# GpSimd makes the low part of more norm pieces, in a two-block float32 model on one core

## What is computed

```python
# first block
h = rmsnorm(x, norm_mix_g);  z = h @ w_in            # MIX
x = x + mixer(z) @ w_out
h = rmsnorm(x, norm_ffn_g)                           # FFN
x = x + (silu(dwconv(h @ w_gate)) * (h @ w_up)) @ w_down
x = rmsnorm(x, norm_final_g)                         # FIN1
# second block: modulate(h, shift, scale) = h * (1 + scale) + shift
h = modulate(rmsnorm(x, g0), shift0, scale0)         # POOL
x = x + gate0 * pool_mixer(h)
hk = modulate(rmsnorm(x, kv_g), shiftkv, scalekv)    # KV
k, v = hk @ w_kv
h = modulate(rmsnorm(x, g1), shift1, scale1)         # ATT, the same x
x = x + gate1 * attention(h @ b_w_in, k, v)
out = rmsnorm(x, final_g)                            # FIN2
```

## Time and profile before

| what | value |
|---|---|
| median of 3 runs | 2089.77 us (2089.43 to 2089.9) |
| the profiled execution's own time | 2088.51 us |
| its span, first to last instruction | 2086.8 us |
| TensorE busy | 2064.3 us |
| VectorE busy | 1231.7 us |
| GpSimd busy | 748.9 us |
| ScalarE busy | 650.7 us |
| mean granted TensorE clock | 0.996 |

### The profile page before, as it was taken

The page is one execution under the profiler, slowest core; times in us unless marked ns, Lnnn a source line. Parts: engine busy times, 40 slices in busy tenths (PEclk is TensorE's granted clock), DMA queues, the critical chain, the costliest instruction groups (busy, mean ns, idle before and its releaser), DMA issues.

```text
span 2086.8 us, 24768 instructions
## 1 busy us (share of the span) xinstructions
PE 2064.3 (99%) x9344; PEld 1694.1 (81%) x9344; DVE 1231.7 (59%) x1698; ACT 650.7 (31%) x1089; POOL 748.9 (36%) x441
## 2 busy tenths in 40 slices
PE   8999999999999999999999999999999999999998
PEld 7888888888888888888878888888888878777886
DVE  7999776555644456445676453453463570697565
ACT  7323345221122211222254122122121261676112
POOL 4555626222221222212276122122131462565623
PEclk9999999999999999999999999999999999999999
DMA  4231112322133222332112121121121120010202
GB/s 154 72 111 41 41 51 91 121 101 97 63 111 111 101 85 76 109 112 101 41 41 61 38 64 41 41 60 40 40 61 41 41 71 31 21 42 21 71 11 81
DMA packets 44749, 141.26 MB, mean 68 GB/s; under 512 B 5616, under 2 KB 9856, under 8 KB 44672
## 3 DMA queue, kind: packets, MB, share of 16 engines
q1 hardware_dynamic: 31632, 100.68, 15.1%
q10 hardware_dynamic: 13040, 39.54, 5.2%
HBM read 135.98 MB, written 7.36 MB: 69 GB/s over the span
## 4 chain that ended last, share of the span: by engine, by line
PE 80%; DVE 12%; POOL 4%; ACT 2%; issue 1%; DMA 0%; POOLq 0%; SPq 0%; ACTq 0%; DVEq 0%
PE psum L594 24%; PE psum L596 24%; PE psum L595 24%; DVE psum L1651 7%; POOL temp L444 2%; PE psum L932 1%; PE psum L943 1%; DVE psum L1504 1%; DVE norm_lo L1517 1%; POOL w_lo L409 1%; PE psum L911 1%; PE psum L661 1%; POOL ada_raw L444 0%; PE psum L663 0%; PE psum L662 0%
## 5 line engine op out<-in xcount | busy, mean ns | idle before, releaser
L409 POOL TENSOR_TENSOR w_lo<-w_raw,w_hi 128x1024 fp32r<-128x1024 f32 x174 | 441.6, 2554 | 972.5 <-ACT w_hi L1036 967.0
L594 PE MATMUL psum<-norm_hi,w_hi 128*128 128x512 f32 x1632 | 636.3, 390 | 0.3 <-ACT temp L1104 0.3
L596 PE MATMUL psum<-norm_hi,w_lo 128*128 128x512 f32 x1632 | 635.0, 389 | 0.0
L595 PE MATMUL psum<-norm_lo,w_hi 128*128 128x512 f32 x1632 | 634.9, 389 | 0.0
L594 PEld LDWEIGHTS psum<-norm_hi,w_hi 128*128 128x128 f32 x1632 | 306.4, 188 | 64.7 <-issue 0.9
L596 PEld LDWEIGHTS psum<-norm_hi,w_lo 128*128 128x128 f32 x1632 | 306.4, 188 | 63.8
L595 PEld LDWEIGHTS psum<-norm_lo,w_hi 128*128 128x128 f32 x1632 | 306.4, 188 | 63.3 <-issue 0.2
L1104 ACT ACTIVATE temp<-psum 128x512 f32<-128x512 f32 x160 | 93.9, 598 | 420.6 <-PE psum L596 393.7
L1567 DVE SCALAR_TENSOR_TENSOR stream<-psum,mods,stream 128x512 f32<-128x512 f32 x160 | 119.7, 750 | 172.5 <-PE psum L596 172.5
L1036 ACT CAST w_hi<-w_raw 128x1024 fp32r<-128x1024 f32 x158 | 159.2, 1047 | 138.8 <-PE psum L596 79.6
L1565 DVE TENSOR_TENSOR stream<-psum,stream 128x512 f32<-128x512 f32 x176 | 118.7, 689 | 83.8 <-PE psum L596 83.6
(11 more groups left out here) (214 smaller groups left out, 2974.7 us busy)
## 6 DMA issues: line engine op xcount, KB each, us to landing
w_raw<-in_slabs SPq DMA_DIRECT2D x175, 512.0 KB, 3.5
ada_raw<-in_ada ACTq DMA_DIRECT2D x10, 3072.0 KB, 12.6
stream<-in_x SPq DMA_DIRECT2D x8, 512.0 KB, 9.3
out<-stream SPq DMA_DIRECT2D x8, 512.0 KB, 2.8
skew_scratch<-row_scratch ACTq DMA_DIRECT2D x1, 3072.0 KB, 17.6
ada_raw<-in_ada ACTq DMA_DIRECT2D x1, 2048.0 KB, 7.9
bias<-skew_scratch ACTq DMA_DIRECT2D x4, 512.0 KB, 4.2
c_act<-in_c ACTq DMA_DIRECT2D x1, 512.0 KB, 9.7
```

The costliest lines, as they stand in the source:

```text
L409: nc.gpsimd.tensor_tensor(WL[place][:, :], RAW[at % 2][:, :], WH[place][:, :].bitcast(f32), ALU.subtract).then_inc(slab_ready, 1)
L594: nc.tensor.matmul(dst, wh, xh, start=n == 0, stop=False)
L595: nc.tensor.matmul(dst, wh, xl, start=False, stop=False)
L596: last = nc.tensor.matmul(dst, wl, xh, start=False, stop=n == len(terms) - 1)
```

## The change

GpSimd takes more pieces: FFN 7, 9, 11, 13, 15 in place of 9, 11, 13; POOL and KV 7, 9, 11, 13, 15 in place of 9, 12, 15; ATT 1, 3, 5, 7, 9, 11, 13 in place of 1, 4, 10, 13. VectorE loses as many `low` instructions. GpSimd's list is reordered to fit: piece 7 stands ahead of the first slab low part that used to come before any piece.

```diff
-        POOL_LOWS = [(MIX, m) for m in (2, 4, 6, 9, 11, 13)] + [(FFN, m) for m in (9, 11, 13)] + [(POOL, m) for m in (9, 12, 15)]
-        POOL_LOWS += [(KV, m) for m in (9, 12, 15)] + [(ATT, m) for m in (1, 4, 10, 13)]
+        POOL_LOWS = [(MIX, m) for m in (2, 4, 6, 9, 11, 13)] + [(FFN, m) for m in (7, 9, 11, 13, 15)]
+        POOL_LOWS += [(POOL, m) for m in (7, 9, 11, 13, 15)] + [(KV, m) for m in (7, 9, 11, 13, 15)]
+        POOL_LOWS += [(ATT, m) for m in (1, 3, 5, 7, 9, 11, 13)]
@@
             sums(FFN)
-            lows(FFN_SLAB + 2, FFN_SLAB + 4)
-            piece_low(FFN, 9)
-            piece_low(FFN, 11)
-            piece_low(FFN, 13)
+            lows(FFN_SLAB + 2, FFN_SLAB + 3)
+            piece_low(FFN, 7)
+            lows(FFN_SLAB + 3, FFN_SLAB + 4)
+            for m in (9, 11, 13, 15):
+                piece_low(FFN, m)
             lows(FFN_SLAB + 4, FFN_SLAB + 6)
@@
             sums(POOL, (f_lo, FT + 1))
+            piece_low(POOL, 7)
             lows(POOL_SLAB + 2, POOL_SLAB + 3)
             piece_low(POOL, 9)
+            piece_low(POOL, 11)
             lows(POOL_SLAB + 3, POOL_SLAB + 4)
-            piece_low(POOL, 12)
+            piece_low(POOL, 13)
             piece_low(POOL, 15)
@@
             sums(KV)
+            piece_low(KV, 7)
             lows(ATT_SLAB + 2, ATT_SLAB + 3)
             piece_low(KV, 9)
+            piece_low(KV, 11)
             lows(ATT_SLAB + 3, ATT_SLAB + 4)
-            piece_low(KV, 12)
-            piece_low(KV, 15)
-            piece_low(ATT, 1)
+            for n, m in ((KV, 13), (KV, 15), (ATT, 1), (ATT, 3)):
+                piece_low(n, m)
             lows(ATT_SLAB + 4, ATT_SLAB + 5)
-            piece_low(ATT, 4)
+            piece_low(ATT, 5)
+            piece_low(ATT, 7)
             lows(ATT_SLAB + 5, ATT_SLAB + 6)
-            piece_low(ATT, 10)
-            piece_low(ATT, 13)
+            for m in (9, 11, 13):
+                piece_low(ATT, m)
             lows(ATT_SLAB + 6, ATT_SLAB + 8)
```

## The result

| | before | after |
|---|---|---|
| median of 7 runs | 2089.77 us (2088.66 to 2092.22) | 2097.0 us (2095.58 to 2098.22) |
| ratio after to before, 95% interval | | 1.0033 (1.0023 to 1.0043) |
| profiled execution, span | 2086.8 us | 2095.3 us |

The account below looks back on a forecast made before the run. TensorE, busy 2064.3 of 2086.8 us, bounds the kernel, so added waits move the end. Losses of 0 (FFN), 2.35 (POOL) and 3.97 us (KV and ATT) sum to 6.3 us: 2096.1 us, 8-in-10 range 2094.3 to 2099.0.

Parts of the forecast that it names:

- GpSimd's queue: POOL, KV, ATT: pieces at 2.37 us and slab low parts at 2.36 us make TensorE wait; losses 2.35 and 3.97 us.
- the five that were named: TensorE waits for GpSimd's low parts at POOL 9 and 13, KV 9 and 13, ATT 5; about 7 us in all.
- the copy: ScalarE's copy to gate_raw before ATT step 8, delayed behind GpSimd's piece 7; TensorE's wait grows from 0.8 to about 1.5 us.
- FFN's zero: FFN: without a shift a piece costs 1.30 us and fits under two steps (2.73 us), so cost and gain are nothing.
- VectorE's relief: Nine fewer VectorE instructions of 0.75 us, 6.8 us less work; buys nothing, as VectorE was already ahead of TensorE.
- The tile read hidden by 0.1 us: After POOL: ScalarE's first FIN1 tile read, late through slab 99's load, ends just before TensorE needs the bank; up to +0.4 us.
- the bound on the gain: With GpSimd free of charge all five waits of before, one of them for gate_raw, go: at most 3.3 us, 2086.5 us.
- GpSimd keeping up: Rival: a whole piece costs about 1.5 us on GpSimd, all five waits of before go, 2086.5 us; chance 0.06.
- The price at which GpSimd would just keep up: POOL before step 13: four pieces and two slabs fit if a piece costs 1.84 us or less.
- Swallowed: Rival: something later has unseen slack and one stage's loss (2.4 us) goes, 2093.7 us; chance 0.08.
- A fall of the clock: Rival: new waits lower TensorE's clock after the last wait of POOL or ATT, +2.2 us each, 2098.3 to 2100.5; chance 0.08.
- A collision with VectorE: Rival: VectorE and GpSimd slow each other, up to 2.0 us per collision, 2098 us with one on the chain; chance 0.04.

Follow-up runs that it names:

- small_slabs: The changed kernel with low parts of slabs 96, 97 and 152 to 155 made for only 32 of 1024 columns; 2087.34 us against 2090.22 before, ratio 0.9985.
- no_shift_add: The changed kernel without the shift addition in GpSimd's POOL, KV and ATT pieces, output not the reference's; 2088.28 us, ratio 0.9991 to the kernel before.
- four_places: The changed kernel with four SBUF places instead of two for GpSimd's pieces in KV and ATT; 2096.22 us, ratio 1.0029 to the kernel before.
- ffn_only: The kernel before with only the FFN part of the change (pieces 7, 9, 11, 13, 15 on GpSimd); 2089.68 us against 2089.69, ratio 0.9999.

## Why the prediction held

**The bound and the place.** As predicted, TensorE had nothing to hide a wait behind, and later stages gave none of it back: shown by the parts that add up, and by the stretch between turn 0 and KV, which was the same to 0.05 us in all twelve profiles.

**GpSimd's queue.** Predicted: POOL +2.35, measured +2.27; KV and ATT +3.97, measured +3.98. The steps that wait are the five that were named and the copy. For the copy the prediction had the path right in all but its last link. It let hi(12) wait for VectorE's scaled(12); in the trace VectorE's scaled(9), held up by GpSimd's piece 5, set hi(9) going, and from there ScalarE ran its four pieces and the copies without a gap. Scaled(12) was done at 1716.37, 0.2 us before hi(12) began. The wait was 1.58 us, 1.65 by the forecast.

```profile
1712.58 0.73 ACT L1082 ACTIVATE norm_hi<-probs,mods 128x512 fp32r<-128x512 f32 x1 [1.98 <-DVE probs L1510]
...
1716.58 0.69 ACT L1082 ACTIVATE norm_hi<-psum,mods 128x512 fp32r<-128x512 f32 x1
1717.17 0.59 ACT L1110 ACTIVATE gate_raw<-psum 128x512 f32<-128x512 f32 x1
```

The cause is shown from both sides: without the slab work (small_slabs) or with a cheap piece (no_shift_add) all waits for GpSimd go; with more places for VectorE (four_places) they stay. FFN's zero was right.

**VectorE's relief** was worth nothing, as forecast. Its busy time fell by 8.8 us where 6.8 were forecast: the nine instructions are 6.6 of it, and six additions at L1664 of before, near 142 to 232 us, took 4.2 us in place of 8.3, as they did in ffn_only, whose first stage was not edited either; other lines took some back.

**Size.** 2096.1 was forecast, 2097.0 measured, and the parts measured one by one give 6.4 us where the sum had 6.3. The remaining 0.9 us of the median lies within what runs of one kernel differ by (2088.66 to 2092.22 for the kernel before), so its cause stays open. The span of the profiled execution was to be 2093.1 us and was 2095.3; the two stretches that vary (turn 0 and the last norm) are 2.0 of the 8.5 us between the two profiled executions. I had not put a term for them, as I took the 0.3 us wait in turn 0 for a fixed figure; it was 0.3 to 1.3 us in the twelve profiles.

**The covers.** The tile read hidden by 0.1 us stayed hidden in the changed kernel, and came out in no_shift_add with 0.59 us, where TensorE was early. No run passed the bound on the gain, 3.3 us (small_slabs had 2.9 of it by the median, 2.25 in its two stretches), but its working was wrong in one term: it lets all five waits go with a fast GpSimd, and the one for the copy stayed in small_slabs and no_shift_add, with 0.5 and 0.7 us. It went only where the copies were moved, or where another wait took its place (four_places).

**The rivals.** GpSimd keeping up: no, 2.37 us for a piece stood. The "about twice" of the Trainium skill's GPSIMD Engine Reference, section 4.1 (Engine selection), fits a subtraction alone (1.29 us on GpSimd; 0.69 us on VectorE, L1515, median of 23) but not the piece, which is two instructions on GpSimd. The price at which GpSimd would just keep up was put too high, at 1.84 us: that looks at step 13, and takes the start of this step from a trace in which TensorE had already waited twice. Step 9 is the tighter one, with two pieces and one slab before it: (1069.26 - 1063.90 - 2.36) / 2 = 1.50 us. At 1.5 us the rival would have been on the edge; no kernel with such a price was run (no_shift_add has 1.26). Swallowed: no. A fall of the clock from the new waits: no. Between 1055 and 1083 us and between 1673 and 1729 us the granted clock was 1.00 (the column behind GpSimd's busy time), with TensorE busy 90% of the time:

```profile
1055.00:1083.00 28.00, 25.12 (x115) 20.18 (x114) 17.76 (x28) 17.26 (x26) 21.23 (x16) 1.00 0.13 38
1673.00:1729.00 56.00, 50.48 (x221) 39.75 (x220) 38.52 (x56) 35.88 (x55) 45.72 (x34) 1.00 0.19 59
```

A collision with VectorE: no. In KV and ATT, with GpSimd busy without a break from its first piece on (the 5.1 us of idle time stand before that piece), the means of before are the same within 5 ns:

```profile
L429 POOL TENSOR_TENSOR norm_lo<-probs,norm_hi 128x512 fp32r<-128x512 f32 x12 | 15.5, 1289 | 0.9
L427 POOL TENSOR_TENSOR probs<-probs,mods 128x512 f32<-128x512 f32 x12 | 12.5, 1043 | 5.1 <-ACT norm_hi L1082 5.1
L1523 DVE SCALAR_TENSOR_TENSOR norm_lo<-psum,mods,norm_hi 128x512 fp32r<-128x512 f32 x15 | 11.1, 745 | 1.1 <-ACT norm_hi L1082 0.9
```

## What to carry to other kernels

Work moved from a fast engine to a slow one must fit, together with all else in that engine's queue, under the pace of the engine that waits for it: add up start-to-start times of the whole queue and compare result by result with when each is wanted. An idle share says little: GpSimd was 36% busy and still too late, while the relieved VectorE only waited longer. And before a piece is handed over later, ask when its input is ready, and what else shares the engine behind it: a wait removed in one stage can return at the next fixed point, as the copy before ATT's step 8 showed.

## What the runs showed of the hardware that I had not expected

The 24 one-column matmuls of the last statistics (L1020, L1026) took 2.81 us in the kernel before and 3.93 in the changed one, and between 2.81 and 4.54 us over the twelve profiles, with the same instructions. They stand behind a wait of 1.28 us in both. In the kernel before they ran from 2073.45 to 2076.26 us, and the granted clock was 1.00 up to 2076 and 0.50 from 2077 on:

```profile
2075.00:2076.00 1.00, 1.00 (x11) 1.00 (x11) 0.00 (x0) 0.00 (x0) 0.00 (x0) 1.00 0.00 0
2077.00:2078.00 1.00, 1.00 (x6) 1.00 (x7) 0.02 (x1) 0.26 (x1) 0.00 (x0) 0.50 0.00 0
```

In the changed kernel they ran from 2080.87 to 2084.80 us, and the clock was at 0.50 before they were done:

```profile
2081.00:2082.00 1.00, 1.00 (x11) 1.00 (x11) 0.00 (x0) 0.97 (x2) 0.00 (x0) 1.00 0.00 0
2083.00:2084.00 1.00, 1.00 (x6) 1.00 (x7) 0.00 (x0) 0.00 (x0) 0.00 (x0) 0.50 0.00 0
```

So TensorE goes down from 2.4 to 1.2 GHz in that thinly filled stretch, in one execution behind these matmuls and in the other among them. That the moment differs from execution to execution, and that it decides their time, was only read from the rows, not tested. Waits of up to 1.6 us inside the full norm stages did not lower the clock (1.00 in the rows above).
